# Attention heads of a hybrid encoder step: scores placed between the second and third transposed piece of a unit, and the first two copies ahead of the scalar engine's softmax work

## The reference

```python
def forgetting_attention(q, k, v, cq, ck, q_pos, k_pos):
    s = jnp.einsum('bqhd,bkhd->bhqk', q, k).astype(jnp.float32) * ATTN_SCALE
    s = s + jnp.swapaxes(cq, 1, 2)[..., :, None] - jnp.swapaxes(ck, 1, 2)[..., None, :]
    s = jnp.where(k_pos[None, :] <= q_pos[:, None], s, NEG_INF)
    p = jax.nn.softmax(s, axis=-1)
    return jnp.einsum('bhqk,bkhd->bqhd', p.astype(v.dtype), v)

def stick_breaking_attention(q, k, v, q_pos, k_pos):
    z = jnp.einsum('bqhd,bkhd->bhqk', q, k).astype(jnp.float32) * ATTN_SCALE
    seen = k_pos[None, :] < q_pos[:, None]
    log_1m_beta = jnp.where(seen, jax.nn.log_sigmoid(-z), 0.0)
    tail = lax.cumsum(log_1m_beta, axis=3, reverse=True) - log_1m_beta
    a = jnp.where(seen, jnp.exp(jax.nn.log_sigmoid(z) + tail), 0.0)
    return jnp.einsum('bhqk,bkhd->bqhd', a.astype(v.dtype), v)
```

## Time and profile before

| | us |
|---|---|
| median of three runs | 1285.31 |
| lowest and highest | 1282.55, 1295.34 |
| the profiled execution | 1286.77 |
| its span, first to last instruction | 1285.2 |
| heads stage in it | 350.4 to 689.5 |

### The profile page before, as it was taken

How to read it: one execution, slowest core, us unless ns; L and a number is a source line. 1 busy time by engine, 2 the same in 40 slices (tenths; PEclk the granted TensorE clock), 3 DMA queues, 4 the chain that set the end, 5 groups by cost and what they waited for, 6 DMA issues and landing times. The chain is left out here.

```text
span 1285.2 us, 19690 instructions
## 1 busy us (share of the span) xinstructions
PE 1210.6 (94%) x7464; PEld 953.8 (74%) x7464; DVE 610.7 (48%) x1095; ACT 504.7 (39%) x1073; POOL 127.2 (10%) x195
## 2 busy tenths in 40 slices
PE   6999999999989989988887999789999999999998
PEld 4878888888656655655556888659999999986886
DVE  4734673310245555579687334473333333343543
ACT  5623222221355555567566433343222222213221
POOL 2000000000000000000005300021111111004321
PEclk9999999999999999999899999889999999999999
DMA  8623445414185556463428985278778878745531
GB/s 295 211 66 95 141 119 147 139 51 158 53 297 175 196 179 183 127 222 123 112 80 267 255 271 183 78 222 304 251 268 275 274 244 269 269 146 171 194 115 49
DMA packets 101979, 233.65 MB, mean 182 GB/s; under 512 B 23190, under 2 KB 50849, under 8 KB 95756
## 3 DMA queue, kind: packets, MB, share of 16 engines
q1 hardware_dynamic: 79212, 166.50, 38.6%
q0 software_dynamic: 16160, 53.50, 14.2%
q10 hardware_dynamic: 6528, 12.58, 3.7%
HBM read 174.70 MB, written 59.81 MB: 182 GB/s over the span
## 5 line engine op out<-in xcount | busy, mean ns | idle before, releaser
L1864 PE MATMUL moe_gu<-moe_xT,moe_room 128*128 128x208 f32 x1024 | 187.5, 342 | 0.6 <-ACT moe_xT L1992 0.6
L438 PE MATMUL zp<-w_low,x_high 128*128 128x512 f32 x432 | 175.7, 407 | 11.8 <-DVE w_low L586 9.5
L1864 PEld LDWEIGHTS moe_gu<-moe_xT,moe_room 128*128 128x128 f32 x1024 | 181.4, 192 | 2.5 <-ACT moe_xT L1992 0.9
L438 PE MATMUL zp<-w_high,x_low 128*128 128x512 f32 x432 | 172.0, 398 | 0.0
L438 PE MATMUL zp<-w_high,x_high 128*128 128x512 f32 x432 | 171.7, 398 | 0.0
L521 ACT ACTIVATE z<-zp,ssx 128x512 f32<-128x512 f32 x54 | 37.1, 688 | 205.7 <-PE zp L438 205.7
L1033 PE MATMUL heads_turn<-ident,heads_prob 128*128 128x128 f32 x596 | 89.1, 283 | 23.9 <-ACT heads_probT L1109 22.9
L438 PEld LDWEIGHTS zp<-w_low,x_high 128*128 128x128 f32 x432 | 81.9, 190 | 32.5 <-DVE x_low L581 11.4
L1109 ACT ACTIVATE heads_probT<-heads_turn 128x512 f32<-128x512 f32 (+1 forms) x131 | 69.6, 548 | 80.3 <-PE heads_turn L1033 80.1
L438 PEld LDWEIGHTS zp<-w_high,x_high 128*128 128x128 f32 x432 | 82.0, 190 | 19.9
L438 PEld LDWEIGHTS zp<-w_high,x_low 128*128 128x128 f32 x432 | 82.1, 190 | 17.8
(11 more groups left out here) (354 smaller groups left out, 2131.7 us busy)
## 6 DMA issues: line engine op xcount, KB each, us to landing
moe_room<-in_w_gu SPq DMA_DIRECT2D x16, 2048.0 KB
moe_room<-in_w_ed POOLq DMA_DIRECT2D x16, 1024.0 KB, 11.2
scratch_grouped<-z POOLq DMA_DIRECT2D x32, 416.0 KB, 26.5
scratch_grouped<-moe_y SPq DMA_DIRECT2D x15, 832.0 KB
h<-in_w_in ACTq DMA_DIRECT2D x24, 512.0 KB, 4.8
scratch_qkT<-ring SPq DMA_DIRECT2D x36, 256.0 KB, 2.7
heads_ckT<-in_cache_kT SPq DMA_DIRECT2D x9, 1024.0 KB, 5.0
heads_cv<-in_cache_v SPq DMA_DIRECT2D x9, 1024.0 KB, 4.9
```

What stands on the lines that cost most here:

```text
L438: mm = pe.matmul(zp[:, U % 3, :], xs[:, k, n * P:n * P + P], ws[g % 2][:, k, :], start=(k == 0 and i == 0), stop=(k == KD - 1 and i == 2))
L1864: mm = pe.matmul(gu[:, u, side, BS * f:BS * f + BS], wgu[u][:, k, DE * side + P * f:DE * side + P * f + P], xT[u][:, k, :], start=(k == 0 ...
```

## The change

On TensorE, turn of unit x is cut in two. Its first two pieces now stand at the start of a step, ahead of the scores of unit x+2; its third and fourth piece stay where they were, behind scores and back. On ScalarE and VectorE the copies of a unit's first two pieces now stand ahead of the step's exponents, sigmoids, biases and scans; later pieces are copied between and behind them as before. `late_copy` is gone. In a step whose unit x+2 is a stick unit VectorE still does its write of x-2 first. The arithmetic, the instructions themselves and the buffers stay; only their order changes.

```diff
-                def turn(U):
-                    for G in range(piece0[U], piece0[U + 1]):
+                def turn(U, begun):
+                    middle = min(piece0[U] + 2, piece0[U + 1])
+                    for G in range(middle, piece0[U + 1]) if begun else range(piece0[U], middle):
...
                 for x in range(NU + 2):
+                    if x < NU:
+                        turn(x, False)
                     if 0 < x and x + 2 < NU:
                         scores(x + 2)
                     if 0 <= x - 2:
                         back(x - 2)
                     if x < NU:
-                        turn(x)
+                        turn(x, True)
                     if 0 <= x - 1 < NU:
                         values(x - 1)
...
                 for x in range(NU + 1):
                     mine = [G for G in range(piece0[x], piece0[x + 1]) if not by_dve[G]] if x < NU else []
+                    while mine and mine[0] < piece0[x] + 2:
+                        copy(mine.pop(0))
                     for e in two:
-                        late_copy = x + 2 < NU and not soft(x + 2)
-                        if mine and not late_copy:
-                            copy(mine.pop(0))
                         if x + 2 < NU and e in parts(x + 2):
                             start(x + 2, e)
-                        if mine and late_copy:
+                        if mine:
                             copy(mine.pop(0))
...
                     if 0 <= x - 2 and ahead and not soft(x + 2):
                         write(x - 2)
+                    while mine and mine[0] < piece0[x] + 2:
+                        copy(mine.pop(0))
                     for e in two:
```

## The result

| | before | after |
|---|---|---|
| median of four runs, us | 1284.18 | 1266.67 |
| lowest and highest | 1282.55, 1295.34 | 1262.3, 1269.1 |
| the profiled execution | 1286.77 | 1266.51 |
| its span | 1285.2 | 1264.9 |

The ratio is 0.9844, with a 95% interval of 0.9815 to 0.9873: the change makes the kernel 1.6% faster.

The account below looks back on a forecast made before the run. TensorE, busy 94% of the span, was taken as the bound, with 40 us idle in the heads. Soft stage 8.6, stick stage 8.8 and clock 5.7 made 23.1 us off 1286.8: 1263 us, range 1255 to 1279.

Parts of the forecast that it names:

- first rival: Second stick pair: the clock's fall to half speed stays, so 5.7 us are not won; 1269 us, chance 0.24.
- Part 1: Soft units: the third or fourth piece's 25 waits of 0.25 us for a copy go, -6.3 us.
- Part 2: Soft units: back's wait for the copy it reads goes, as transposes now lie between, -2.6 us.
- Part 3: Soft units: half of TensorE's 6.5 us wait for VectorE to read the score tile goes, -3.2 us.
- Part 4: Soft units: new wait of the next unit's second piece for the bank of a three-piece unit's last, +3.5 us.
- Part 5: Stick units: copies leave the place between sigmoids; pairs one and two and single head win 3.4, 3.6 and 1.8 us.
- VectorE's cap: Stick units: VectorE's busy time plus three us of gaps holds pair one to about 42.0 us, pair two to 43.4.
- Part 6: Block's tail: SyncE's wait for the last mixing load sets the end, so TensorE's gain there is lost, 0 us.
- Part 7: Second stick pair: the clock's fall to half speed goes as waits shrink, -5.7 us.
- The slower rival: Heads: second pieces wait for late copies at every unit with a third piece, net +16 us; 1295 us, chance 0.05.

Follow-up runs that it names:

- turn-only kernel: Changed kernel with TensorE's new order alone, ScalarE's and VectorE's copies as before the change: 1318.88 us, 1.0243 of the kernel before.
- third-piece kernel: Changed kernel with ScalarE's copy of the third piece also ahead of the first exponent in steps with soft x+2: 1259.49 us, ratio 0.9786.
- the change run again: Changed kernel, unaltered, measured a second time: 1266.12 us, 0.9833 of the kernel before.
- seam copy: Changed kernel with all pieces of the last soft unit copied by ScalarE: 1266.15 us, 0.9833 of the kernel before.
- the last kernel: The kernel of all three edits, with the second half of `w_out` also loaded ahead of the last head's loads: 1254.3 us, ratio 0.975.
- all three edits: Changed kernel with third-piece copy ahead of the exponent, last soft unit's copies on ScalarE, and small router loads early: 1255.71 us, ratio 0.975.
- the early loads: Changed kernel with router weights, bias and `norm_ffn_cols` loaded ahead of the last head's own loads: 1263.65 us, 0.9827 of the kernel before.
- The two halves of the change: Changed kernel with only TensorE's new order, 1318.88 us; changed kernel with only ScalarE's and VectorE's copies moved, 1335.83 us.

## Why the prediction was right, and where it was not

**The sum.** Forecast 1263, measured 1266.7, and 0.9833 to 0.9844 of the kernel before in two groups against the 0.983 forecast. The time lies between the forecast and its first rival (the clock's fall stays, 1269), and somewhat nearer to the rival. The terms say the same: the order gave a little more than forecast, and the 5.7 us of the clock were not won. That the total is so close to 1263 is in part luck, as these two misses go against each other.

**Parts 1 to 3** name the waits that went. Part 1: 24 of the 25 waits are gone. (Its 1.7 us for unit 5's scores is 1.83 by the rows that it cites; nothing hangs on it.) Part 2: 2.6 us became 0.6. Part 3: 6.5 us became 1.3, so 5.2 went where I took half. The rows alone don't show that VectorE's early copy is what part 1 rests on; the turn-only kernel does.

**Part 4** had the right mechanism, shown by the third-piece kernel, and was too small: 5.6 us of waits against 3.5. The largest, 1.76 us, is at the start, where a unit of four pieces makes the next one wait; Part 4's condition asked for three. The other six come to 3.8 us. Parts 2 to 4 miss in both directions, and that the soft stage still comes out at the -8.6 forecast, 203.0 to 194.5 in the change run again, is luck. The profile shown above has 196.1, with a fall of the clock at 354.6 to 357.7 us that the other doesn't have.

**Part 5.** The sigmoids are the new limit, at 8.3 us against "about 8". VectorE's cap was too pessimistic: 42.1 us in pair two against 43.4, and -3.7 against -1.8 in the single head. The failed step of this part is that I read VectorE's 15.3 busy us in the single head's window as work that had to be done inside it. The window is cut at TensorE's marks, and VectorE runs behind TensorE; what is late at the cut is passed on. VectorE is now busy for 12.88 us there and for 14.91 in the tail, before it was 15.34 and 13.10. Pair one, -3.4 forecast, came out at +0.8, 46.2 us. With the seam copy and at a clock of 1.00 it takes 42.8 (the last kernel), near the 42.0 forecast. So 3.4 us are the copy at the seam and the fall of the clock together. At a like clock of 0.96 the seam copy takes 1.1 to 1.8 us off pair one (45.5 us with the third piece ahead, 44.4 with all three edits, 43.7 with the seam copy), so about half of the 3.4 is the seam. I didn't look for it: the prediction went through places inside a pair and none where a soft unit meets a stick unit. One of its signs of being wrong, that VectorE is what TensorE waits for in stick units, came true there, and for 0.37 us in the tail.

**Part 6** held: the tail went from 20.8 to 21.1 us and SyncE's last wait from 3.8 to 4.4. TensorE's products end 3.1 us ahead of the block's end and that is lost. Whether issuing or landing holds up the block's end the prediction didn't ask; the early loads answer it.

**Part 7** is the step that failed. "As the waits shrink, I take it that the fall is gone": it left pair two (-10.6 us there, of which the cleaner comparisons above give about five to the order; the rest is the size that Part 7 gave to the fall) and came back in pair one and at the mixing's start, in TensorE's wait for that block. The wait after, the wait before (where no fall came), and the two falls:

```profile
670.22 0.77 PE L1374 MATMUL mix_om<-w_out_low,w_high 128*128 128x512 f32 x1 [5.28 <-DVE w_out_low L1509]
692.22 0.47 PE L1370 MATMUL mix_om<-w_out_low,w_high 128*128 128x512 f32 x1 [2.70 <-DVE w_out_low L1505]
...
552.00:560.00 8.00, 6.76 (x38) 4.24 (x35) 5.23 (x10) 1.90 (x7) 0.00 (x0) 0.57 0.01 1
668.00:676.00 8.00, 5.78 (x15) 4.58 (x16) 7.34 (x12) 7.97 (x16) 7.58 (x25) 0.57 0.67 200
```

The fall at the mixing's start need not be the change's. All thirteen profiles other than that of the kernel before have one there, in or right behind a wait of 2.5 to 5.3 us. The two halves of the change are among them, with 2.50 us, less than the kernel before had. The kernel before has a single profile, and that may be the exception. The sign "the stages behind the heads take longer than 595.7 us" came true too (596.9, where it was 595.2 by the same mark), but says little: with the same arithmetic these stages took 593.1 to 598.2 us in the other profiles, and 604.1 in one.

The mean granted clock is 0.985 before and after, some 38 us at half speed in both spans (twice 0.015 of the span, rounded figures). Over the last group's runs its median is 0.986 for both kernels. The Trainium skill's rule on transposes (TensorE: Matmul & The Clock Gate, Part 4: PE-mode transpose: they do not count as activity the way products do) would have kept the falls where transposes crowd. The soft units turn blocks all the way through, and in the kernel with all edits and half of `w_out` moved their stage has TensorE busy for 185.36 of 188.7 us at a clock of 1.00, 60.7 us of it with transposes. So the traces don't bear the rule out; in the heads and at the mixing's start each fall of the profile after came in or behind a wait of TensorE (1.76, 1.51 and 5.28 us).

**The slower rival** had a real mechanism: the turn-only kernel is 2.4% slower through waits for banks, 36.8 us in 28 waits in the stick units. It needs the copies to be late, and the change moves them.

## What to carry to other kernels

When an engine's steps are cut and moved, move the steps of the engines that free its buffers in the same edit, and don't judge either half by its own run: here they cost 2.4% and 3.8% apart and won 1.6% together. After such a change look for the buffer whose release still stands behind unrelated work (here one copy behind one exponent, 0.5% more), first at the start and at the seams between kinds of steps. Count a fall of the clock as something that moves, not as a gain to be booked, as long as waits like those here, of 0.8 us and more, remain.

## What the runs showed of the hardware

The same waits bring a fall of the clock in one execution and none in another. In the profile after, the wait of 1.51 us at the seam was followed by the fall shown above; in the last kernel the same step had this wait and a clock of 1.00 in each us from 542 to 552:

```profile
545.42 0.28 PE L988 MATMUL score<-identb,mask_stick 128*128 128x128 bf16 x2 [1.51 <-ACT heads_prob L1098]
```

It fell instead in pair two, from 607 to about 610.5, behind waits of 0.82 and 0.75 us, where the profile after has a like couple of waits (at 571.37 and 572.78) in pair one at 1.00 throughout. And the change run a second time had falls at about 555 to 559, 572 to 576 and 616 to 620 us where the first had 552 to 559 alone in the stick pairs. The Trainium skill says that the moment at which the clock rises behind the start of sustained work differs between runs of one kernel (TensorE: Matmul & The Clock Gate, Part 1: The HAM clock gate). These traces show the same of the falls. A fall of this kind costs little: pair two takes 42.1 us at 1.00 and 43.6 or 43.7 at 0.96. One elsewhere can come with more: the profiled execution of all three edits had an additional one in the mixing (750.6 to 760.8 us), behind a wait of 2.07 us; that execution took 1264.1 us, against the median of 1255.7.
